# Twelve of sixteen rows of one adaLN third as running sums on VectorE, added over partitions a whole third at a time

## The reference, cut to what matters

```python
def adaln(c, w, b):
    m = jax.nn.silu(c) @ w + b
    shift, scale, gate = jnp.split(m, 3, axis=-1)
    return shift[:, None], scale[:, None], gate[:, None]
```

## Time and profile before

| | us |
|---|---|
| median of 3 runs | 1330.7 (1329.9 to 1330.9) |
| the profiled execution, its own time | 1330.37 |
| its span, first to last instruction | 1328.5 |
| TensorE busy | 1298.3 (98%) |
| VectorE busy | 785.6 (59%) |
| ScalarE busy | 515.7 (39%) |

### The profile page before, as it was taken

One profiled execution on the slowest core, in us unless ns is written; L12 is line 12 of the kernel. 1 busy time (PEld: TensorE's weight loads), 2 busy tenths in 40 slices (PEclk: granted clock), 3 DMA queues, 4 the chain that ended last, 5 costly groups with the idle time before them and its releaser, 6 DMA issues.

```text
span 1328.5 us, 17027 instructions
## 1 busy us (share of the span) xinstructions
PE 1298.3 (98%) x6611; PEld 1028.5 (77%) x6611; DVE 785.6 (59%) x1131; ACT 515.7 (39%) x880; POOL 62.7 (5%) x80
## 2 busy tenths in 40 slices
PE   5999999999999999999999899999999999999997
PEld 2567777787888878888887688887788888888885
DVE  3334865776767768665885566884444444454445
ACT  4223333343333333353334743333453343433333
POOL 2000100000100020001000100000000000001000
PEclk9999999999999999999999999999999999999999
DMA  9999687745666457544774566663332112216443
GB/s 379 387 403 396 249 311 273 259 138 179 213 225 222 127 189 255 191 142 159 264 245 149 166 226 199 217 223 120 111 111 64 48 65 64 64 49 246 150 153 132
DMA packets 70111, 257.80 MB, mean 194 GB/s; under 512 B 8504, under 2 KB 8632, under 8 KB 68752
## 3 DMA queue, kind: packets, MB, share of 16 engines
q1 hardware_dynamic: 64368, 235.48, 51.1%
q0 software_dynamic: 5520, 21.17, 4.8%
q10 hardware_dynamic: 144, 0.07, 0.0%
HBM read 248.76 MB, written 7.93 MB: 193 GB/s over the span
## 4 chain that ended last, share of the span: by engine, by line
PE 95%; DMA 2%; DVE 1%; issue 1%; ACT 1%; POOL 0%; SPq 0%; ACTq 0%; POOLq 0%
PE gemm L511 20%; PE gemm L513 20%; PE gemm L512 19%; PE attended L705 4%; PE turned L655 3%; PE gemm L483 2%; PE gemm L485 2%; PE gemm L484 2%; PE ada_bank L631 2%; PE scores L953 2%; PE scores L691 2%; DMA ada<-in_ada_all 2%; PE ada_bank L589 1%; PE scores L957 1%; PE scores L655 1%; PE ada_bank L485 1%
## 5 line engine op out<-in xcount | busy, mean ns | idle before, releaser
L1416 DVE TENSOR_TENSOR w_lo<-w_raw,w_hi 128x1024 fp32r<-128x1024 f32 x242 | 294.7, 1222 | 287.2 <-ACT w_hi L1029 286.2
L511 PE MATMUL gemm<-w_hi,act_lo 128*128 128x512 f32 x1146 | 459.8, 401 | 0.5 <-DVE w_lo L1416 0.5
L513 PE MATMUL gemm<-w_hi,act_hi 128*128 128x512 f32 x1146 | 447.5, 390 | 0.0
L512 PE MATMUL gemm<-w_lo,act_hi 128*128 128x512 f32 x1146 | 446.7, 390 | 0.0
L1029 ACT ACTIVATE w_hi<-w_raw 128x1024 fp32r<-128x1024 f32 x242 | 253.8, 1056 | 303.1 <-PE gemm L513 255.8
L511 PEld LDWEIGHTS gemm<-w_hi,act_lo 128*128 128x128 f32 x1146 | 215.4, 188 | 54.9 <-issue 12.6
L513 PEld LDWEIGHTS gemm<-w_hi,act_hi 128*128 128x128 f32 x1146 | 215.1, 188 | 46.6
L512 PEld LDWEIGHTS gemm<-w_lo,act_hi 128*128 128x128 f32 x1146 | 215.6, 188 | 42.1
L1085 ACT ACTIVATE prob<-scores,nmax 128x384 f32<-128x384 f32 (+1 forms) x96 | 48.9, 510 | 103.0 <-DVE nmax L1604 96.7
L1604 DVE TENSOR_REDUCE nmax<-scores 128x1 f32<-128x384 f32 (+1 forms) x96 | 42.6, 465 | 68.9 <-PE scores L957 48.5
L1501 DVE SCALAR_TENSOR_TENSOR ada<-ada,silu_c 128x1024 f32<-128x1024 f32 x60 | 78.8, 1350 | 0.0
(11 more groups left out here) (309 smaller groups left out, 1553.5 us busy)
## 6 DMA issues: line engine op xcount, KB each, us to landing
w_raw<-in_w_all SPq DMA_DIRECT2D x245, 512.0 KB, 3.7
ada<-in_ada_all SPq DMA_DIRECT2D x168, 512.0 KB, 6.7
gate_ring<-in_ada_all SPq DMA_DIRECT2D x24, 512.0 KB, 4.4
gate_bc<-gate_scratch POOLq DMA_DIRECT2D x4, 1024.0 KB, 6.9
st<-x_scratch POOLq DMA_DIRECT2D x4, 768.0 KB, 5.1
x_scratch<-u POOLq DMA_DIRECT2D x3, 768.0 KB, 4.7
u<-in_x_sample SPq DMA_DIRECT2D x2, 1024.0 KB, 8.3
bias<-in_bias_all POOLq DMA_DIRECT2D x2, 1024.0 KB, 8.5
```

The source lines that it names most:

```text
L511: pe.matmul(bank_[:], alo, whi[:, kk], start=first, stop=False)
L512: pe.matmul(bank_[:], ahi, wlo[:, kk], start=False, stop=False)
L513: last = pe.matmul(bank_[:], ahi, whi[:, kk], start=False, stop=end)
L1416: dve.tensor_tensor(w_lo[:, r, 0:width], w_raw[:, r, 0:width], hi_slot(w)[:, 0:width].bitcast(F32), ALU.subtract).then_inc(lo_ready, 1)
```

## The change

Of layer 0's gate third (number 2) rows 4 to 15 become two more running sums of 12 pieces each, ahead of the other four; its first four rows stay visits, so that third takes two visits in place of eight. The second visits' third (number 5) is visited in group 0's units rather than in group 1's plain slots. The places beside which products are done are laid out anew, with two products in many attention units where there was one or none. Accumulators move (`u`, `bias_acc`). The sums over partitions are done once for a whole third, both halves together: three times in place of four.

```diff
 V_RING, P_RING = 3, 4
 SHARED = 4
 V_GATE = KT - SHARED
-SUMS = [(4, 0), (4, 1), (3, 0), (3, 1)]
+SUMS = [(2, 0, SHARED), (2, 1, SHARED), (4, 0, 0), (4, 1, 0), (3, 0, 0), (3, 1, 0)]
 SLICES = KT // KPS
 HALVES = 2 * KT
...
+        bias_acc = sb("bias_acc", [P, 2, 2, CH], F32, at=bias_at)
         halves = ada.rearrange("p r (g n) -> p r g n", g=2)
-        sums_of = [[rows[:, 0:2, :], u[:, 0:2, D - CH:D]], [halves[:, 0], halves[:, 1]],
-                   [halves[:, 2], halves[:, 3]], [rows[:, 0:2, :], late_acc[:]]]
+        u_wide = u[:, 2, D - 2 * CH:D].rearrange("p (g n) -> p g n", g=2)
+        u_last = u[:, 0:2, D - CH:D]
+        sums_of = [[u[:, 0:2, D - 2 * CH:D - CH], u_wide], [rows[:, 0:2, :], u_last],
+                   [halves[:, 0], halves[:, 1]], [halves[:, 2], halves[:, 3]],
+                   [rows[:, 0:2, :], u_last], [bias_acc[:, 0], bias_acc[:, 1]]]
         nmax = sb("nmax", [P, 4]); rsum = sb("rsum", [P, 4]); rinv = sb("rinv", [P, 4])
         assert top[0] <= nc.sbuf_usable_end, top[0] - nc.sbuf_usable_end
...
         block = ctx.enter_context(nc.Block())
 
         VISIT = 4
-        P_THIRDS = [(2, KT), (5, SHARED)]
-        visits = {W_A + 2 * q + 1: (0, q) for q in range(SPC)}
-        for q in range(SHARED // 2):
-            visits[W_A + 2 * SPC + 3 + 2 * q] = (1, q)
-        p_first = [0, 2 * KT, 2 * (KT + SHARED)]
+        P_THIRDS = [(2, SHARED), (5, SHARED)]
+        visits = {W_A + 1: (0, 0), W_A + 3: (0, 1), W_A + SPC + 1: (1, 0), W_A + SPC + 3: (1, 1)}
+        p_first = [0, 2 * SHARED, 4 * SHARED]
         P_END = p_first[-1]
 
 
-        sums_in_a = {5: 0, 6: 1}
-        sums_in_b = [{j: KT + n for n, j in enumerate(j for j in range(2, 23) if j % 4 != 1)},
-                     {j: 2 * KT + 4 + n
-                      for n, j in enumerate((2, 3, 4, 5, 6, 7, 8, 9, 11, 13, 15, 16, 18, 19, 20, 22))}]
-        sums_in_units = {n: 2 * KT + (n - 2) // 2 for n in range(2, 10)}
-        sums_in_out = {SPC * i + j: 3 * KT + 4 + 6 * (i - 1) + n
-                       for i in (1, 2) for n, j in enumerate((0, 1, 2, 4, 5, 6))}
-        sums_at = [W_A + i * 2 * SPC + j for i in range(N_A) for j in (5, 6, 8, 9, 11, 12, 13, 15)]
-        sums_at += [W_B + j for j in sums_in_b[0]] + [W_B + 3 * SPC + j for j in (2, 3, 5, 6)]
-        sums_at += [W_B + 4 * SPC + j for j in sums_in_b[1]]
-        sums_at += [W_O0 + j for j in sums_in_out]
-        V_END = len(SUMS) * KT
+        sum_first = [0]
+        for _, _, k0 in SUMS:
+            sum_first.append(sum_first[-1] + KT - k0)
+        V_END = sum_first[-1]
+        sums_at = []
+        slot_sums, unit_sums = {}, {}
+
+        def sums_beside_slots(w0, places):
+
+            for j in places:
+                slot_sums[w0 + j] = len(sums_at)
+                sums_at.append(w0 + j)
+
+        def sums_beside_units(group, w0, count):
+
+            for h in range(2 * count):
+                n = 1 + h * (UNITS - 1) // (2 * count)
+                unit_sums.setdefault((group, n), []).append((len(sums_at), h % 2))
+                if h % 2 == 1:
+                    sums_at.append(w0 + n * SPC // UNITS)
+
+        for i in range(N_A):
+            sums_beside_slots(W_A + i * 2 * SPC, (4, 5, 6) if i == 0 else (0, 4, 5, 6))
+            sums_beside_units(i, W_A + i * 2 * SPC + SPC, 9)
+        sums_beside_slots(W_B, range(2, 3 * SPC - 1))
+        sums_beside_units(N_A, W_B + 3 * SPC, SPC)
+        sums_beside_slots(W_B + 4 * SPC, list(range(2, 16)) + [17, 19, 21])
+        sums_beside_slots(W_O0, (5, 6, 7))
+        for i in (1, 2):
+            sums_beside_slots(W_O0 + i * SPC, (0, 1, 2, 4, 5, 6))
+        sums_beside_slots(W_O0 + 3 * SPC, (0, 1))
         assert len(sums_at) == V_END
+        V_MOVED = slot_sums[W_B + 4 * SPC + 14]
         gate_sums_at = [W_QL + j for j in range(6, 2 * SPC)] + [W_G + j for j in range(4, SPC)] \
             + [W_G + SPC + j for j in (0, 1, 2, 4, 5, 6)] + [W_G + 2 * SPC + j for j in range(4)]
...
-            def part_sums(part):
+            def third_sums(n):
 
                 pe.wait_ge(column_set, 1)
-                pe.wait_ge(v_used, KT * (part + 1))
-                need(pe, rows_free, ROWS_0 + 2 + part)
-                add_partitions(AD, SUMS[part][1], [[a[:, gg, :] for gg in range(2)] for a in sums_of[part]])\
-                    .then_inc(summed, 1)
+                pe.wait_ge(v_used, sum_first[2 * n + 2])
+                need(pe, rows_free, ROWS_0 + 2 + n)
+                for half in range(2):
+                    vectors = sums_of[2 * n + half]
+                    if (n, half) == (2, 0):
+                        vectors = [vectors[0], late_acc[:]]
+                    last = add_partitions(AD, half, [[a[:, gg, :] for gg in range(2)] for a in vectors])
+                last.then_inc(summed, 1)
 
             def gate_sums():
 
...
                         score(n0 + 1, 0, 1, 0)
                     chunk_slot((w0 + j), j % SPC, m + (NT * (j // SPC)))
-                    if j == 0:
-                        part_sums(i)
-                    if i == 1 and j == 19:
-                        part_sums(2)
+                    if (i, j) in ((0, 0), (1, 5)):
+                        third_sums(i)
                     ada_visit(w0 + j)
...
             for i in range(N_OUT - 1):
                 for j in range(SPC if i < N_OUT - 2 else SPC - LAST):
                     chunk_slot((W_O0 + SPC + j + i * SPC), j, (M_O0 + NT + i * NT))
-                    if i == N_OUT - 2 and j == 0:
-                        part_sums(3)
                     if i == N_OUT - 2 and j == 2:
-                        pe.wait_ge(rows_free, ROWS_0 + 6)
+                        third_sums(2)
+                    if i == N_OUT - 2 and j == 4:
+                        pe.wait_ge(rows_free, ROWS_0 + 5)
...
                 act.wait_ge(kb_out, 16 * (i + 1))
                 need(act, t_done, tau + 2 * GROUP)
-                if i == N_B - 1:
+                if i == 0:
                     act.wait_ge(rows_free, ROWS_0 + 3)
+                else:
+                    act.wait_ge(v_used, V_MOVED + 1)
                 w_gate = w
                 for n in range(UNITS):
...
-                if first:
+                if before is None:
                     return dve.tensor_scalar(out, slot, scalar, None, ALU.mult)
-                return dve.scalar_tensor_tensor(out=out, in0=slot, scalar=scalar, in1=out,
+                return dve.scalar_tensor_tensor(out=out, in0=slot, scalar=scalar, in1=before,
                                                 op0=ALU.mult, op1=ALU.add)
 
             def part_product(at, v):
 
-                part, k = at // KT, at % KT
+                part = [n for n in range(len(SUMS)) if at >= sum_first[n]][-1]
+                n = at - sum_first[part]
                 slot = v_ring[:, at % V_RING, :].rearrange("p (g n) -> p g n", g=2)
+                out = sums_of[part][v]
+                before = None if n == 0 else out
                 if v == 0:
                     landed(dve, v_in, at)
                     need(dve, v_used, at)
-                    if part == 3 and k == 0:
+                if part == 4 and v == 1 and at >= V_MOVED:
+                    out = late_acc[:]
+                    if at > V_MOVED:
+                        before = out
+                    else:
                         need(dve, t_done, T_B + T_B_PER + 2 * GROUP)
-                last = add_product(sums_of[part][v], slot, k, v, k == 0)
+                last = add_product(out, slot, SUMS[part][2] + n, v, before)
                 if v == 1:
                     last.then_inc(v_used, 1)
+
+            def slot_products(w):
+
+                if w in slot_sums:
+                    for v in range(2):
+                        part_product(slot_sums[w], v)
+
+            def unit_products(group, n):
+
+                for at, v in unit_sums.get((group, n), []):
...
                     if not 1 <= j < 4:
                         split_lo(W_A + j + 2 + i * (2 * SPC))
-                    if j in sums_in_a:
-                        for v in range(2):
-                            part_product(i * SPC + sums_in_a[j], v)
+                    slot_products(W_A + i * 2 * SPC + j)
+                    if i == 0 and j == 5:
+                        add_rows(2, p_first[1])
                 for n in range(UNITS):
                     if n + 2 < UNITS:
                         maximum(n0 + (n + 2), (n + 2) % NT)
...
                         output(n0 + (n - 1), (n - 1) % NT, i * CH + (n - 1) // NT * P)
                     for j in beside(n):
                         split_lo(W_A + SPC + j + 2 + i * (2 * SPC))
-                    part_product(i * SPC + 2 + n // 2, n % 2)
-                    if i == 1 and n == 4:
+                    unit_products(i, n)
+                    if i == 0 and n == 7:
                         add_rows(5, P_END)
                 output(n0 + (UNITS - 1), NT - 1, i * CH + (GROUP - 1) * P)
-                if i == 0:
```

(16 more changed lines are left out.)

36 lines of the change are left out of this document (17 added, 19 removed).

## The result

The changed kernel takes 1338.3 us in the median of four runs (1337.9 to 1338.3), beside 1330.8 of the kernel before: a ratio of 1.0057 with a 95% interval of 1.0041 to 1.0073. It is 7.5 us slower; 4.5 were forecast. The profiled execution took 1338.32 us, its span is 1336.5.

What follows compares the result with a forecast made beforehand. TensorE, busy 98% of the span, was taken as the bound. Taking 14.4 us off it against 18.9 lost where VectorE is late gave +4.5 us on 1330.37, 1334.9, so a median of 1335.2 us; range 1326.5 to 1339.

Steps and rivals of the forecast that it cites:

- the likeliest case: VectorE sets the pace in the named places of loss; 68%, own range 1332 to 1338 us.
- Removed from TensorE: Six visits at 2.05 us, 12.3 us, and three whole sums for four half ones, 2.05: together 14.4 us.
- Group A's plain slots: VectorE's added products delay the copies of turned queries: 1.6 us lost in the first group, 5.7 in the second.
- the forecast's chain: VectorE's queue in A's second group's plain slots: norms, three `split_lo`, three pairs, two copies, second copy ending at 270.4.
- Units: VectorE slower than TensorE: lost 1.0 us in A's first group, 3.3 in its second, 3.7 in group B's first units.
- The rate of 13.2 us for three units: Group A's second group: two more products make VectorE take 13.2 us per three units, against TensorE's 12.12.
- Plain slots of group B: A `split_lo` and a pair, 3.54 us, fit into slots of 4.1 us: 0 lost.
- Rival (c): GpSimd's mask in group B slows products beside it until TensorE waits for `w_lo`: 1337 to 1340 us; 10%.
- The second output chunk: The pair ahead of the residual delays a `split_lo` to 644.0 where TensorE wants the slot at 641.88: lost 2.1 us.
- rival (d): Waits of 1.5 to 2.5 us drop TensorE's clock, one slot taking 8.2 for 4.1: 1339 us and up; 3%.
- The last sum: Last chunk: VectorE's products end at 712.8, TensorE finishes slot 2 at 711.3: lost 1.5 us.

Runs made afterwards that it cites:

- moved pair: Changed kernel with one pair of products moved from slot 7 of the first output chunk to slot 3 of the next: 1334.6 us, ratio 1.0029.
- later sum: Changed kernel with the moved pair and the whole sum of the last third behind slot 3 of the last chunk, not slot 2: 1333.1 us.
- units: Changed kernel without the products of ten pieces beside attention units (three of nine in each group of A, four of eight in group B's first): 1329.8 us.
- the kernel with that part alone: Kernel before with both halves of one third added at once in group B's second group, no visit gone, no product added: 1328.5 us, ratio 0.9985.
- the two visits: Kernel before without layer 1's two gate-third visits in group A's second group and their loads, nothing added to VectorE: 1327.4 us, ratio 0.9977.
- version with seven visits: Complete version with six of the gate third's sixteen rows as running sums and the last sum behind slot 3: 1322.3 us, ratio 0.9940 to the kernel before.
- The changed kernel's second trace: The changed kernel run once more with nothing changed: median 1338.0 us, ratio 1.0055, profiled execution 1336.69 us.
- the rows added later: Later-sum kernel (1333.1) with VectorE's adding of rows moved from unit 7 of group A's first group to unit 4 of its second: 1333.0 us.

## Why the prediction was right, point by point

**The sign and the reason.** The time lies 3.1 us above the forecast of 1335.2 and inside the range of 1326.5 to 1339, but 0.3 outside the 1332 to 1338 that the likeliest case had for itself. VectorE sets the pace in the places named, and the loss exceeds the gain. The three tests that take one place's load away (moved pair, later sum, units) give back 3.7, 1.5 and 8.5 us; the terms of the sum for them were 2.1, 1.5 and 8.0. Of the 3.7 the low stretch is 1.7, and part of the 8.5 can be the same: by the shifts the units give back 7.6.

**Removed from TensorE.** 14.3 us by the shifts against 14.4: a visit 2.05, a whole sum no dearer than a half one (the kernel with that part alone).

**Group A's plain slots.** 1.6 and 5.7 measured, as forecast. In the first group the added products make all of it. In the second they make 2.9 (the forecast's steps for the two new pairs there are 0.6 and 2.4), and the other 2.8 are lost without them: three visits, 6.2 us, are gone, and VectorE's older chain has room for 3.4. Take the two steps out of the forecast's chain and its second copy ends at 267.4, 3.4 us ahead of TensorE's third turn at 270.80: it had both the size and the division. The expectations of the later runs didn't see that, and put all 5.7 down to the added products first, then all but 0.7 of the two visits down to the old chain.

**Units.** 1.2, 3.8 and 4.4 against 1.0, 3.3 and 3.7. The rate of 13.2 us for three units was right (13.17). What is left, 0.5 and 0.7 us, would be slack that was assumed too large at the start of a block; no row was read for it. Of the first group's 1.2 half goes with the adding of rows, which the forecast left out of these units, and the rest with products. The version with seven visits, with one product in a unit but two in the first and the addition elsewhere, loses nothing there.

**Plain slots of group B.** 0 was forecast, 0.0 measured. Rival (c) is refuted: the pair beside GpSimd's mask again takes long, 6.84 us where the one ahead of it takes 2.47, and TensorE has no wait between 314.51 and 443.35 nor between 470.94 and 598.06, where the plain slots of both groups lie. VectorE's and GpSimd's rows of the changed kernel:

```profile
494.25 6.84 DVE L1527 SCALAR_TENSOR_TENSOR ada<-ada,silu_c 128x1024 f32<-128x1024 f32 x2
...
493.54 5.27 POOL L2138 TENSOR_TENSOR bias<-bias,mask 128x2048 f32<-128x2048 f32 x1 [9.18 <-DMA bias<-in_bias_all]
```

**The second output chunk: the mis-sized term.** "Lost 2.1" was 3.9 in the profiled execution. The wait was right (2.00); what the sum left out stood in rival (d), at 3%, as a whole case: TensorE at the lower level of its clock behind a wait. It came as an addition of 1.7 us behind one wait. The changed kernel's second trace, with the wait and without the low stretch, is 1.6 us shorter, and the shift at 722.4 is +6.28 in place of +7.94. That execution took 1336.7, inside the likeliest case's own range of 1332 to 1338. That low stretches stand behind some waits of this length, and go when the wait goes, is shown; what decides when isn't.

"TensorE: Matmul & The Clock Gate" of the Trainium skill (What's actually happening) has the clock fall when the engine was idle, by a monitor that looks at its activity on a beat of its own, not on the kernel's. The trace agrees in that between 140 and 720 us the lower level stands only behind a wait of this length, and not behind each: behind 2.11 at 263.15 and 1.94 at 457.65 of this trace the clock stayed at 1.00. That the beat decides between them, no run here shows.

**The last sum.** 1.5 forecast and 1.50 measured, and one slot later it is free.

## What to carry to other kernels

Work moved from the engine that is the bound to one that is busy 59% gains only at the places where the second engine has time between two of its deadlines; lay its queue against the first one's place by place, and put the added work where the slots have room. Here twelve rows placed everywhere cost 7.5 us, and six rows in the roomy places gained 8.4, of which 2.1 come from adding both halves at once. Work taken off the bound engine is worth nothing beyond the room of the other one's old chain behind it: there it was 3.4 us, whether 4.1 or 6.2 had been taken off. Count that room before the gain.

## What the hardware showed that was not expected

TensorE's clock fell to its lower level behind a single wait of about 2 us in some executions and not in others, for the same wait at the same place. The traces of the changed kernel and of its variants have eighteen waits of 1.9 us or more in TensorE's queue between 140 and 720 us. Behind four of them stands a low stretch: behind the 2.00 at 646.63, behind the 2.10 at the second group's turned queries in the kernels with the later last sum and with the rows added later, and behind the 1.95 at 458.70 in the latter. None stands in that stretch without such a wait, nor in the versions that have no wait of that length. Two windows, first of the kernel with the later last sum, then of the one with the rows added later:

```profile
262.00:272.00 10.00, 9.25 (x38) 7.20 (x39) 8.07 (x12) 4.26 (x11) 0.00 (x0) 0.83 0.56 200
```

```profile
260.00:280.00 20.00, 17.89 (x83) 13.74 (x83) 14.93 (x21) 8.33 (x19) 0.00 (x0) 0.91 0.56 184
```

What it costs depends on who sets the pace there: 1.7 us at the output chunk, where TensorE does so at once, and 0.3 behind 262.75, where VectorE is the later one for most of the time. There the shift grows by 0.90 between 225.3 and 290.6 with the low stretch (-3.58 to -2.68) and by 0.62 without it, in the kernel with the moved pair alone (-3.31 to -2.69).
